# Reordering VectorE's work at the seams between two sublayers of a four-layer transformer

## The reference, cut to what matters

```python
for layer in range(DEPTH):
    u = rms_norm(h, norm_g[layer, 0])
    u = mixer(u, ...)
    h = h + rms_norm(u, norm_g[layer, 1])
    u = conv_ffn(rms_norm(h, norm_g[layer, 2]), ...)
    h = h + rms_norm(u, norm_g[layer, 3])
```

## Time and profile before

| | |
|---|---|
| median of 3 runs | 2615.09 us (2614.69 to 2615.44) |
| the profiled execution | 2615.86 us, its span 2614.1 us |
| mean granted TensorE clock | 0.997 |
| TensorE matmul busy | 98% of the span |
| VectorE busy | 62% |
| ScalarE busy | 45% |
| GpSimd busy | 14% |

### The profile page before, as it was taken

One profiled execution on the slowest core, in us unless ns is written; L12 is line 12 of the kernel. 1 busy time (PEld: TensorE's weight loads), 2 busy tenths in 40 slices (PEclk: granted clock), 3 DMA queues, 4 the chain that ended last, 5 costly groups with the idle time before them and its releaser, 6 DMA issues.

```text
span 2614.1 us, 38319 instructions
## 1 busy us (share of the span) xinstructions
PE 2551.6 (98%) x13432; PEld 2152.9 (82%) x13432; DVE 1630.7 (62%) x2821; ACT 1171.1 (45%) x1799; POOL 359.3 (14%) x322
## 2 busy tenths in 40 slices
PE   8999999999999999999999999999999999999997
PEld 6999978888878677888878878888779998788886
DVE  6588667664252847667256676673386885766733
ACT  4367544443232845444235554443343774544421
POOL 2011121110010522111010021110010111211100
PEclk9999999999999999999999999999999999999999
DMA  4410023333233022332321123333333001233231
GB/s 156 142 33 1 26 81 97 96 96 98 81 109 97 17 65 89 97 96 90 106 79 62 41 81 103 96 97 97 94 113 105 9 2 49 89 97 97 88 105 48
DMA packets 61907, 210.90 MB, mean 81 GB/s; under 512 B 8528, under 2 KB 10320, under 8 KB 61776
## 3 DMA queue, kind: packets, MB, share of 16 engines
q1 hardware_dynamic: 61776, 209.13, 26.0%
HBM read 207.01 MB, written 2.10 MB: 80 GB/s over the span
## 4 chain that ended last, share of the span: by engine, by line
PE 90%; DVE 7%; ACT 1%; issue 1%; POOL 0%; DMA 0%; SPq 0%; DVEq 0%; ACTq 0%; POOLq 0%
PE psum L304 21%; PE psum L306 21%; PE psum L305 21%; PE psum L1077 6%; PE psum L1065 3%; PE psum L906 3%; PE psum L908 3%; PE psum L907 3%; PE psum L1055 2%; PE psum L1054 2%; DVE xl L477 2%; DVE h L494 2%; PE psum L338 1%; DVE dh L493 1%; PE psum L332 1%
## 5 line engine op out<-in xcount | busy, mean ns | idle before, releaser
L304 PE MATMUL psum<-xh,w_hi 128*128 128x512 f32 x1712 | 667.0, 390 | 0.1
L305 PE MATMUL psum<-xh,w_lo 128*128 128x512 f32 x1712 | 666.1, 389 | 0.0
L306 PE MATMUL psum<-xl,w_hi 128*128 128x512 f32 x1712 | 666.1, 389 | 0.0
L266 DVE TENSOR_TENSOR w_lo<-w_raw,w_hi 128x1024 fp32r<-128x1024 f32 x226 | 280.3, 1252 | 513.5 <-ACT w_hi L260 511.2
L260 ACT ACTIVATE w_hi<-w_raw 128x1024 fp32r<-128x1024 f32 x226 | 236.2, 1057 | 564.9 <-PE psum L306 455.1
L304 PEld LDWEIGHTS psum<-xh,w_hi 128*128 128x128 f32 x1712 | 321.4, 188 | 66.8 <-issue 0.6
L306 PEld LDWEIGHTS psum<-xl,w_hi 128*128 128x128 f32 x1712 | 321.3, 188 | 66.8
L305 PEld LDWEIGHTS psum<-xh,w_lo 128*128 128x128 f32 x1712 | 321.4, 188 | 66.4
L698 DVE TENSOR_TENSOR w_lo<-w_raw,w_hi 128x1024 fp32r<-128x1024 f32 x160 | 209.3, 1308 | 253.7 <-ACT w_hi L694 253.7
L304 PE MATMUL psum<-ah,w_hi 128*128 (+1 forms) x704 | 273.9, 389 | 0.0
L305 PE MATMUL psum<-ah,w_lo 128*128 (+1 forms) x704 | 273.9, 389 | 0.0
(11 more groups left out here) (198 smaller groups left out, 3837.4 us busy)
## 6 DMA issues: line engine op xcount, KB each, us to landing
w_raw<-w_up SPq DMA_DIRECT2D x176, 512.0 KB, 3.6
w_raw<-w_down SPq DMA_DIRECT2D x88, 512.0 KB, 3.6
w_raw<-nsa_in SPq DMA_DIRECT2D x56, 512.0 KB, 3.7
w_raw<-sb_in SPq DMA_DIRECT2D x24, 512.0 KB, 3.7
w_raw<-nsa_out SPq DMA_DIRECT2D x16, 512.0 KB, 3.7
w_raw<-swa_in SPq DMA_DIRECT2D x10, 512.0 KB, 3.7
w_raw<-sb_out SPq DMA_DIRECT2D x8, 512.0 KB, 3.7
w_raw<-swa_out SPq DMA_DIRECT2D x8, 512.0 KB, 3.7
```

Source lines behind the costliest of these rows:

```text
L266: nc.vector.tensor_tensor(w_lo[:, u % RING, :], w_raw[:, u % RING, :], w_hi[:, u % RING, :].bitcast(F32), ALU.subtract).then_inc(split_don ...
L304: nc.tensor.matmul(bank(p, o), wh[:, k, o, :], xhi(k), start=(first and k == 0), stop=False)
L305: nc.tensor.matmul(bank(p, o), wl[:, k, o, :], xhi(k), start=False, stop=False)
L306: mm = nc.tensor.matmul(bank(p, o), wh[:, k, o, :], xlo(k), start=False, stop=(last and k == 1))
```

## The change

The order in which VectorE works at the seven inner seams is altered. The low part of chunk 3 follows right behind the weights' low part. The full update of h's chunk 0 moves from there to between the low part of chunk 5 and the update of chunk 7. Three waits of VectorE on its own h_done go with the loop. ScalarE's order of squares follows: 1, 2, 3, 4, 5, 6, 0, 7. As chunk 0 of u is now read after xh's chunks 4 to 6 have been written over ffn_u, the stored chunks of u are rotated by one slot: chunk 0 lies in slot 3, chunk 1 in slot 0, and so on. The number of instructions of every kind, and what each computes, stays as it was, and so does every transfer.

```diff
+        def u_slot(c):
+            return (c + 3) % 4
+
         def dve_take_u(dve, s, p, u):
...
-                nc.vector.tensor_copy(u[:, o, :], bank(p, o)).then_inc(u_done, 1)
+                nc.vector.tensor_copy(u[:, u_slot(o), :], bank(p, o)).then_inc(u_done, 1)
...
-                    src, d = u[:, c, :], dh[:, c % 2, :]
+                    src, d = u[:, u_slot(c), :], dh[:, c % 2, :]
...
             low(2)
             split_lo(dve, u_split)
+            low(3)
+            update(4)
+            update(5)
+            low(4)
+            update(6)
+            low(5)
             update(0)
-            for c in range(4, DC):
-                dve.wait_ge(h_done, 8 * s + c)
-                update(c)
-                low(c - 1)
-            low(DC - 1)
+            update(7)
+            low(6)
+            low(7)
             dve.sem_inc(evac_v, 1)
...
-            for k, c in enumerate((1, 2, 3, 0, 4, 5, 6, 7)):
+            for k, c in enumerate((1, 2, 3, 4, 5, 6, 0, 7)):
                 act.wait_ge(h_done, 8 * s + k + 1)
```

More of the change, by code:

```diff
@@ L508, in dve_update @@
                 dve.wait_ge(r_done, 2 * s + a + 1)
-                m = ch.then(nc.vector.scalar_tensor_tensor(dh[:, 0, half], u[:, 0, half], gg[:, s:s + 1], rn[:, half], ALU.mult, ALU.mult))
+                m = ch.then(nc.vector.scalar_tensor_tensor(dh[:, 0, half], u[:, u_slot(0), half], gg[:, s:s + 1], rn[:, half], ALU.mult, ALU.mult))
                 dve.wait_ge(hg_done, s + 1)
```

## The result

| | before | after |
|---|---|---|
| median | 2615.09 us (5 runs, 2614.69 to 2616.01) | 2627.56 us (5 runs, 2625.26 to 2628.50) |
| profiled execution, its span | 2615.86, 2614.1 | 2625.26, 2623.4 |
| mean granted clock of the five executions after | | 0.995, 0.994, 0.993, 0.993, 0.994 |

The ratio is 1.0045, 95% interval 1.0032 to 1.0058: slower by 12.5 us, where +5.2 was forecast in a range that ended at 2626.5. The direction was right, the size too small.

A forecast was written before the change was run, and what follows sets the result against it. TensorE was taken to bound the kernel, waiting for VectorE's low parts at seven seams. Waits gained and update 0's price summed to +0.74 us a seam, +5.2 us in all: 2620.3 us, range 2611.5 to 2626.5.

The forecast's parts named there:

- What bounds the kernel: TensorE holds 90% of the chain; ahead of line 338 it waits 21.5 us for VectorE's low parts, at seven seams.
- Gained first: Chunk 3's low part, ahead of any GpSimd add, ends at 365.71; TensorE's wait for it until 369.14 goes.
- GpSimd's start: GpSimd's first add at 368.53; chunk 4's low part leads by 0.10 us, runs unblocked, and TensorE's wait for it goes.
- Rival B: GpSimd gets in before chunk 4's low part: line 385 +1.5 us a seam, 2625.5 us; chance 0.20.
- Update 0 at its new place: Behind chunk 5's low part, GpSimd's adds hold up both halves of update 0: 3.4 us for what took 1.5.
- Rival A: Update 0 is not held up and costs 1.5 us at its new place: 2600 to 2607 us; chance 0.13.
- low(6): Chunk 6's low part: GpSimd ahead by 0.03 us, end at 378.84; one TensorE wait of 2.6 us replaces three.
- Rival C: VectorE wins the 0.03 us tie at chunk 6's low part: -0.3 us a seam, 2613 us; chance 0.11.
- The end: TensorE from chunk 6's low part to line 385: reached at 382.80 against 382.06, +0.74 us a seam.

The follow-up runs named there:

- small_adds_after: The changed kernel with GpSimd's adds of h's squares at the seven inner seams cut to 16 of 512 tokens: 2602.08 us, ratio 0.9948.
- wait_in_two: The changed kernel with TensorE also waiting for update 0 before chunk 6's first matmul, ahead of its wait for chunk 6's low part: 2620.97 us, ratio 1.0020.
- update5_high7: The kernel before with chunk 3's low part directly behind update 0, and TensorE taking chunk 7's high part ahead of chunk 6's low part: 2604.88 us, ratio 0.9959.
- update5_first: The kernel before with chunk 3's low part moved directly behind update 0, ahead of update 4, and the three h_done waits dropped: 2607.43 us, ratio 0.9967.

## Why the prediction was wrong in size

*What bounds the kernel* was right: TensorE's order, and VectorE's low parts ahead of line 338, in all seven seams.

*Gained first*, right: low(3) at 0.74 and no wait at chunks 3, 4 and 5.

*GpSimd's start*, right, and the bound left open there is narrowed from one side: a lead of 0.11 us is enough for VectorE. Rival B falls.

*Update 0 at its new place*, right: 1.78 and 1.66 us, 3.39 from issue to the next instruction's start (371.62 to 375.01) against the forecast 3.4. Rival A falls, and with it what the Trainium skill (Advanced Engine Details and Errata, VectorE Performance Modes) would have made of it: small adds turn the loss to a gain, so the two exclude each other outside any two-port mode.

*low(6)*, right: GpSimd ahead by some 0.02 us (376.38 against 376.39), low(6) at 1.80. Rival C falls. So small a lead need not have held: the one kind of meeting that VectorE won at such a lead is that of small_adds_after.

*The end* is the step that failed. It took the instructions behind the wait, "with 1.19 (as behind the wait at 375.41), then 1.81 and 0.91 for chunk 7", at the durations that followed the kernel before's short waits, which held TensorE up by 1.1, 0.4 and 0.4 us (369.14 against 368.08, and steps of 3.14 and 3.13 us to 372.28 and 375.41 where the work is 2.74). The sum of +0.74 a seam was measured at +0.75 wherever the clock stayed up, and wait_in_two puts the total of that term at 5.1 us. But behind a single wait of 2.5 us the granted clock fell, in three seams of the profiled execution and in up to five by the times of others (an estimate), at 1.58 us each: 4.7 to 7.9 us, as much again as the whole forecast. No rival carried that term, so the range ended at 2626.5, a microsecond short of the median. It could have had a bound from the trace of before. There, at the start of each seam, TensorE waits 1.9 us for the first xh, and behind one of these seven waits the clock falls; the stretch of the fifth seam in the kernel before (the granted clock again third from the end):

```profile
1515.00:1547.00 32.00, 29.77 (x127) 23.36 (x126) 26.76 (x34) 17.60 (x30) 9.85 (x7) 0.95 0.15 48
```

It cost nothing there, as the waits for low(3) to low(5) were still ahead and took it up. A longer wait with dense work behind it had to be given the price of a fall in each seam as its upper bound.

Open is which of the seams fall. In both profiled executions of the changed kernel the first two did not. Seams 3 and 7 (in the other 3 and 6) had a fall at the seam's start instead, and their waits for low(6) were then only 1.3 to 1.5 us; that they kept the clock there agrees with the rest. The runs show that the length of the wait decides whether a fall can happen, not what picks among the seams with the long one, nor what picks the falls at a seam's start.

## What to carry to other kernels

Before moving an instruction of VectorE with two SBUF inputs, look at what GpSimd does at the new place, not at the old: here 1.4 us of work became 3.4. When several short waits of TensorE become one long one, price the clock besides the wait, and prefer an order that cuts the wait in pieces; an added wait gained 5 us here. And where every instruction's time and the rule of who goes first are known from the trace, try neighbouring orders on paper: moving low(3) by one place and leaving update 0 alone gave -8 us where the proposed order gave +12.

## What the runs showed of the hardware

- Wherever a VectorE instruction of the seam with two SBUF inputs and a GpSimd add met, one of them was held (low parts 0.75 to 1.8 us, the add 1.3 to 1.8), while all those with one input in PSUM kept 0.75 and 0.69. The one that started first went first, down to leads of 0.11 us (VectorE) and 0.02 us (GpSimd). Where both starts read the same, the outcome differs: a full add went ahead of low(4) at 370.75 in update5_high7, VectorE's add ahead of a small add at 371.19 in small_adds_after, there in all seven seams. What decides such a tie is open. With both always waiting they alternate, and VectorE's back-to-back instructions do not keep GpSimd out: at 371.62 and 373.43 both halves of one update were held up.
- TensorE's clock fell to half behind single waits of 2.5 us (3 of 5, in each of three profiled executions) and of 3.2 us (4 of 7), and never behind a pair of 1.2 and 1.0 us or a wait of 1.5 us at that place (5 each). Behind the wait of 1.9 us at a seam's start it fell in one or two of seven seams in 11 of the 13 profiled executions, the one before included, and in none in the other two.
- What a fall costs is a matter of what stands behind it: 1.58 us where TensorE's work is dense, nothing in the kernel before and the changed one at a seam's start, where later waits take it up (27.51 us against 27.52), 0.2 us in update5_first, 0.6 in update5_high7, and 1.0 at the same place in the changed kernel with small adds, which has no such waits (25.76 against 24.74).
- Where the clock does not fall behind low(6), the stretch of the changed kernel repeats within 0.08 us over seven seams and two profiled executions, that of the kernel before within 0.03, so that differences of 0.3 us in one seam could be forecast and found.
